# A last chunk of a recurrence and the output projection behind it: two tiles split by token halves, queues reordered

## The chip, the core and the metric

One Trainium2 chip, one of its cores. The metric is the device time of one execution in microseconds (us). TensorE multiplies, VectorE and ScalarE work elementwise and read TensorE's results out of PSUM, GpSimd works on SBUF only, SyncE issues the transfers. Each engine has a queue of its own and takes its instructions strictly in the order in which they are written; between engines only semaphores order the work.

## What is computed

A trunk of two layers on 576 tokens: 64 of a running stream, then 512 of a new one. Cut to the part around the change, for each layer:

```python
proj = rmsnorm(x) @ w_in                     # 1024 -> GLA columns and RWKV columns
o = gla_chunked(q, k, v, log_a, state)       # 4 heads, chunks of 64 tokens, a recurrence over chunks
o = o * rsqrt(mean(o * o) + eps) * gla_norm_w * silu(gg)
y = rwkv7(r, w, k, v, -kk, kk * a, state)    # 8 heads of 64, also a recurrence
y = (y - mean(y)) * rsqrt(var(y) + gn_eps) * ln_w + ln_b
y = (y + bonus) * g
x = x + concat([o, y]) @ w_out               # 1024 -> 1024: the output projection
x = x + conv_ffn(rmsnorm(x))
```

## The kernel before

Everything lies transposed: 128 features on the partitions, the 576 tokens along the free dimension. A dense product takes 128 output features at a time, a tile. Tiles alternate between two slots, s = 0 and 1, each with its weights and its two banks of PSUM (PS[0], PS[1]); a bank holds half of the tokens, HT = 288. Weights and inputs are split into a high and a low part in fp32r, and a product is three passes: high by high, high by low, low by high (`passes`, L610). A pass is two matmuls, one for each half of the tokens (`both`, L600), each with a weight load of its own. For a tile of 8 blocks of the contraction that is 48 matmuls of 288 columns; L602 is the first half's, L603 the second's.

A tile of weights comes by DMA into `raw`; ScalarE makes the high part `whi` when the slot's last tile is done (L1182, semaphore `tile_done`), then GpSimd the low part `wlo` (L529, `w_lo`), and TensorE waits for `w_lo` (`dense`, L619). In the output projection ScalarE does that in `added` (L1200), beside xh and the squares of the next norm, and VectorE adds the tile to x (L2121).

The mixers run in nine chunks of 64 tokens, 0 to 8 (LAST = 8). The loop over i from -1 to 7 does chunk i's recurrence and, beside it, prepares chunk i + 1: the order of all engines' steps in it is written out by hand. A chunk's recurrence of the RWKV heads is a chain in which TensorE and a reader of PSUM alternate, each a group of 16 matmuls of 64 by 64: `carried` (L845, copied by ScalarE to Zc), `solve_z` (L869; VectorE's `add_z`, L1923, makes Z of it and Zc), `carried_y` (L857), `solve_z1` (L879, copied by ScalarE, L1399, to Z1), `solve_z2` (L887; VectorE's `add_rest`, L1939, makes W), `solve_u` (L895, copied to U), and `outputs` (64 matmuls, L903 to L914), from which VectorE makes the new state (`new_state`, L1952 and L1954) and the chunk's y (`add_y`, L1933).

The two norms go by groups of two chunks: a mean on TensorE (the matmul with `mean64` or `mean128`), logarithm and exp on ScalarE, the scale on VectorE (`scale_o`, L1995; `scale_y`, four instructions, L2003). `mixed_o` and `mixed_y` then write the inputs of the output projection: high part mh by ScalarE (L1461, L1470), low part ml by VectorE (L2011, L2017). Blocks 0 to 3 of the contraction are o, 4 to 7 are y. Semaphores `mo_lo` and `my_lo` count groups. For the last group (chunks 7 and 8) y's norm is taken one chunk at a time: `chunk_mean` (L1017) on TensorE, `chunk_centre` (L2030) on VectorE, `square_chunk` (L1475) and `log_chunk` (L1480) on ScalarE, and one exp for both (L1548).

Where exp and logarithm alternate on ScalarE, a table load stands ahead of the one that changes: it is shown with that one's line (L1446 for the exp of `rstd_o`). At the end of the loop's last pass VectorE does `scale_o` of the last group and its product with the silu (L2078); only then do its steps of chunk 8 follow, from L2086 on. TensorE's order behind the loop is:

```python
carried(LAST); solve_z(LAST); chunk_mean(7, mean); carried_y(LAST)
solve_z1(LAST); solve_z2(LAST); solve_u(LAST)
chunk_mean(7, variance); outputs(LAST)
chunk_mean(8, mean); out_part(0, range(0, 1)); chunk_mean(8, variance)
turn_state(St, zb)
out_part(0, range(1, 4)); out_part(1, range(0, 4))
out_part(0, range(4, 8)); out_part(1, range(4, 8))
```

`out_part(s, kts)` (L1079) does blocks kts of tile s for all tokens. Six more tiles follow with `dense`, then the FFN.

## Time and profile before

| | |
|---|---|
| median of 3 runs | 1687.81 us (1686.81 to 1690.52) |
| the profiled execution | 1688.88 us |
| its span | 1686.5 us |
| TensorE: matmuls | 1642.1 us, 97% of the span |
| VectorE | 934.5 us, 55% |
| ScalarE | 660.7 us, 39% |
| GpSimd | 557.8 us, 33% |
| mean granted clock of TensorE | 0.991 of full speed |
| transfers | 115.38 MB, a mean of 68 GB/s |

The profiled execution is 1.07 us above the median; 2.4 us of it lie outside the span. Busy time is that of instructions with an end that is modelled for TensorE, so neighbouring matmuls overlap in the rows: their starts tell the pace. In a timeline row an idle time in brackets stands for the engine's wait just before, with what ended it. The granted clock is a share of TensorE's full speed: 1.00 is 2.4 GHz, 0.50 is 1.2 GHz.

### The profile page before, as it was taken

The page shows a single profiled execution, that of the slowest core. Times are in us where ns is not written, and L with a number is a line of the kernel's source. Part 1 is how long each engine was busy: PE and PEld are TensorE (multiplying, and loading weights), DVE is VectorE, ACT ScalarE, POOL GpSimd, SP SyncE. Part 2 cuts the span into 40 slices and gives each one's busy share as a digit, 9 for nine tenths or more (in the row PEclk, how much of TensorE's full clock was granted, in tenths as well). Part 3 has the DMA queues.
Part 4 walks back from the last instruction along what each step waited for, and adds up shares of the span by engine and source line. Part 5 has one row for each costly group of instructions (what it writes and reads, how often), then busy time and mean ns, then how long its engine had stood idle before and what let it go on. Part 6 is the DMA issues. An engine that isn't in the chain of part 4 may idle for free.

```text
span 1686.5 us, 40380 instructions
## 1 busy us (share of the span) xinstructions
PE 1642.1 (97%) x18045; PEld 1578.2 (94%) x18045; DVE 934.5 (55%) x1414; ACT 660.7 (39%) x995; POOL 557.8 (33%) x293
## 2 busy tenths in 40 slices
PE   7999999989999999999999999999899999999997
PEld 6999988869999999999999998887799999999997
DVE  4669545555566405665546884465556661266643
ACT  5444345553433213333253533555443331233323
POOL 5434311114344333443333432021134433334331
PEclk9999999999999999999999999999899999999999
DMA  5222210002323322223222222000132233232331
GB/s 150 63 75 76 65 40 4 4 2 82 88 75 88 103 73 75 83 81 104 81 74 75 76 76 58 10 4 3 33 88 78 86 94 94 64 88 77 102 88 57
DMA packets 218861, 115.38 MB, mean 68 GB/s; under 512 B 9332, under 2 KB 216450, under 8 KB 218690
## 3 DMA queue, kind: packets, MB, share of 16 engines
q1 hardware_dynamic: 218610, 112.79, 23.5%
q8 instruction: 143, 2.34, 0.6%
q14 instruction: 28, 0.23, 0.0%
q10 hardware_dynamic: 80, 0.02, 0.0%
HBM read 109.27 MB, written 3.53 MB: 67 GB/s over the span
## 4 chain that ended last, share of the span: by engine, by line
PE 94%; ACT 2%; DVE 2%; issue 1%; DMA 0%; POOL 0%; SPq 0%; DVEq 0%; ACTq 0%
PE ps L602 38%; PE ps L603 38%; PE ps L822 2%; PE ps L825 2%; PE ps L819 2%; PE ps L607 1%; PE ps L785 1%; PE ps L798 1%; PE ps L887 1%; PE ps L943 1%; PE ps L799 1%; PE ps L1004 1%; PE ps L879 1%; PE ps L717 1%; PE ps L961 1%
## 5 line engine op out<-in xcount | busy, mean ns | idle before, releaser
L529 POOL TENSOR_TENSOR wlo<-raw,whi 128x1024 fp32r<-128x1024 f32 (+1 forms) x188 | 508.5, 2705 | 861.7 <-ACT whi L1182 861.6
L1182 ACT ACTIVATE whi<-raw 128x1024 fp32r<-128x1024 f32 (+1 forms) x188 | 209.5, 1114 | 650.1 <-PE ps L603 650.1
L602 PE MATMUL ps<-xh,whi 128*128 128x288 f32 x1120 | 332.8, 297 | 4.2 <-DVE xl L1610 4.2
L603 PE MATMUL ps<-xh,whi 128*128 128x288 f32 x1120 | 331.0, 296 | 0.0
L602 PE MATMUL ps<-xl,whi 128*128 128x288 f32 x1120 | 330.2, 295 | 0.0
L603 PE MATMUL ps<-xl,whi 128*128 128x288 f32 x1120 | 329.0, 294 | 0.0
L602 PE MATMUL ps<-xh,wlo 128*128 128x288 f32 x1120 | 329.0, 294 | 0.0
L603 PE MATMUL ps<-xh,wlo 128*128 128x288 f32 x1120 | 328.9, 294 | 0.0
L602 PEld LDWEIGHTS ps<-xh,whi 128*128 128x128 f32 x1120 | 210.7, 188 | 6.2 <-issue 4.5
L603 PEld LDWEIGHTS ps<-xh,whi 128*128 128x128 f32 x1120 | 210.6, 188 | 0.2
L602 PEld LDWEIGHTS ps<-xh,wlo 128*128 128x128 f32 x1120 | 210.7, 188 | 0.0
L603 PEld LDWEIGHTS ps<-xl,whi 128*128 128x128 f32 x1120 | 210.5, 188 | 0.0
L603 PEld LDWEIGHTS ps<-xh,wlo 128*128 128x128 f32 x1120 | 210.1, 188 | 0.0
L602 PEld LDWEIGHTS ps<-xl,whi 128*128 128x128 f32 x1120 | 210.0, 187 | 0.0
L2121 DVE TENSOR_TENSOR x<-x,ps 128x576 f32<-128x576 f32 x48 | 36.2, 753 | 197.4 <-PE ps L603 197.4
L2159 DVE SCALAR_TENSOR_TENSOR cv<-up,par,cv 128x578 f32<-128x578 f32 x44 | 100.5, 2284 | 32.8 <-ACT cv L1566 32.8
L2174 DVE SCALAR_TENSOR_TENSOR hl<-hf,hh 128x576 fp32r<-128x576 f32 x44 | 98.5, 2239 | 33.3 <-ACT hh L1572 33.3
L603 PE MATMUL ps<-hh,whi 128*128 128x288 f32 x352 | 103.7, 295 | 0.0
L603 PE MATMUL ps<-hl,whi 128*128 128x288 f32 x352 | 103.6, 294 | 0.0
L602 PE MATMUL ps<-hl,whi 128*128 128x288 f32 x352 | 103.5, 294 | 0.0
L602 PE MATMUL ps<-hh,wlo 128*128 128x288 f32 x352 | 103.4, 294 | 0.0
L602 PE MATMUL ps<-hh,whi 128*128 128x288 f32 x352 | 103.4, 294 | 0.0
(301 smaller groups left out, 3156.3 us busy)
## 6 DMA issues: line engine op xcount, KB each, us to landing
raw<-in_ffn_w_up SPq DMA_DIRECT2D x88, 512.0 KB, 3.8
raw<-in_w_in SPq DMA_DIRECT2D x52, 512.0 KB, 3.8
raw<-in_ffn_w_down SPq DMA_DIRECT2D x32, 704.0 KB, 4.5
raw<-in_w_out SPq DMA_DIRECT2D x16, 512.0 KB, 3.8
xin<-in_x_prompt SPq DMA_DIRECT2D x4, 512.0 KB, 6.7
out<-xin SPq DMA_DIRECT2D x8, 256.0 KB, 2.9
out<-RW SPq DMA_DIRECT2D x16, 64.0 KB, 2.2
g<-in_rwkv_g SPq DMA_DIRECT2D x2, 256.0 KB, 2.8
```

What stands on the lines that cost most here:

```text
L529: e.tensor_tensor(wlo[s][:, 0:width], raw[s][:, 0:width], whi[s][:, 0:width].bitcast(F32), ALU.subtract).then_inc(w_lo[s], 1)
L602: e.matmul(acc(out)[:, 0], lhsT, rhs[:, 0:HT], start=start, stop=stop)
L603: return e.matmul(acc(out)[:, 1], lhsT, rhs[:, HT:TOK], start=start, stop=stop)
L607: e.matmul(out[:, 0:512], lhsT, rhs[:, 0:512], start=True, stop=True)
L717: ws = e.matmul(PS[2][:, tt], w2a2[0:64, p * P:(p + 1) * P], R[0:64, 12, tt], start=True, stop=True)
L819: mm = e.matmul(powers[h, X, 0], d[h, hp, X, 2], d[h, hp, X, 0], start=True, stop=True)
L822: mm = e.matmul(powers[h, X, 1], d[h, hp, X, 0], d[h, hp, X, 2], start=True, stop=True)
L825: mm = e.matmul(product[h, X], d[h, hp, X, 2], d[h, hp, X, 1], start=True, stop=True)
L1182: e.activation(whi[s][:, 0:width], raw[s][:, 0:width], ACT.Copy).then_inc(w_hi[s], 1)
L2121: e.tensor_tensor(by_half(xt), by_half(xt), acc(PS[s]), ALU.add).then_inc(psum_free[s], 1)
L2159: e.scalar_tensor_tensor(out=cv[:, :], in0=up[:, 1:3 + TOK], scalar=par[:, cw + FF + f:cw + FF + f + 1], in1=cv[:, :], op0=ALU.mult, op1=A ...
L2174: e.scalar_tensor_tensor(out=hl[:, it, :], in0=hf[:, :], scalar=1.0, in1=hh[:, it, :].bitcast(F32), op0=ALU.mult, op1=ALU.subtract).then_i ...
```

## The change

`out_part` becomes `out_half(s, b, kts)`: blocks kts of tile s for token half b alone. The first halves of tiles 1 and 0 are cut into slices that stand between TensorE's steps of chunk 8; behind the turned state only the second halves are left. A first half needs the groups of chunks 0 to 4 alone. The count of y (`Y`) leaves `dv_b` for a semaphore `dv_a` of its own, so that VectorE can make y ahead of the state. VectorE's `scale_o` and its product, and ScalarE's `rstd_o`, move from the end of the loop into the last chunk; the rest of both queues is put in another order there. Squares of chunks 7 and 8 lie in SQ[:, 1], the mean and the variance of chunk 7 in other banks. The diff, cut where only the name of the semaphore changes:

```diff
@@ -110,7 +110,8 @@
 
 PE_B = ["Zc", "Z", "Yc", "Z1", "Z2", "U", "S"]
 AC_B = ["Zc", "Yc", "Z1", "U"]
-DV_B = ["Z", "W", "Sa", "St", "Y"]
+DV_B = ["Z", "W", "Sa", "St"]
+DV_A = ["Y"]
 
 PE_G = ["scores", "tok", "out", "state"]
 AC_G = ["tok", "oE", "oO"]
...
@@ -130,7 +131,7 @@
 LAST = NCH - 1
 PE_E = ["m7", "v7", "m8", "v8"]
 AC_E = ["s7", "l7", "s8", "l8", "rstd"]
-DV_E = ["c7", "y3b", "y3", "gb", "c8", "gy0", "gy1", "gy2", "gy3", "yr", "y"]
+DV_E = ["c7", "c8", "gy0", "gy1", "gy2", "gy3", "gb", "y3b", "y3", "yr", "y"]
 
 
 def program(nc, x_prompt, x_sample, state_gla, state_rwkv, state_rwkv_shift, cache_ffn_conv,
...
@@ -317,7 +318,7 @@
         st_pe = sem("st_pe")
         st_dve = sem("st_dve")
         pe_f, ac_f, dv_f, po_f = sem("pe_f"), sem("ac_f"), sem("dv_f"), sem("po_f")
-        pe_b, ac_b, dv_b = sem("pe_b"), sem("ac_b"), sem("dv_b")
+        pe_b, ac_b, dv_b, dv_a = sem("pe_b"), sem("ac_b"), sem("dv_b"), sem("dv_a")
         pe_g, ac_g, dv_g = sem("pe_g"), sem("ac_g"), sem("dv_g")
         pe_y, ac_y, dv_c, dv_y, po_y = sem("pe_y"), sem("ac_y"), sem("dv_c"), sem("dv_y"), sem("po_y")
         pe_e, ac_e, dv_e, o_last = sem("pe_e"), sem("ac_e"), sem("dv_e"), sem("o_last")
...
@@ -1076,46 +1077,57 @@
                     level(j, 0, 5)
                     level(j, 1, 5)
 
-                def out_part(s, kts):
-
+                def out_half(s, b, kts):
+
+                    groups = l * len(GROUPS) + (3 if b == 0 else len(GROUPS))
+                    if b == 0 and 0 in kts:
+                        pe.wait_ge(w_lo[s], turn(s, l, PAIRS["out"]) + 1)
                     if 0 in kts:
-                        pe.wait_ge(w_lo[s], turn(s, l, PAIRS["out"]) + 1)
-                        pe.wait_ge(mo_lo, (l + 1) * len(GROUPS))
+                        pe.wait_ge(mo_lo, groups)
                     if 4 in kts:
-                        pe.wait_ge(my_lo, (l + 1) * len(GROUPS))
+                        pe.wait_ge(my_lo, groups)
+                    own = slice(b * HT, (b + 1) * HT)
                     for kt in kts:
-                        mm = passes(s, mh, ml, kt, KT)
-                    if KT - 1 in kts:
+                        wh = whi[s][:, kt * P:(kt + 1) * P]
+                        wl = wlo[s][:, kt * P:(kt + 1) * P]
+                        e.matmul(acc(PS[s])[:, b], wh, mh[:, kt, own], start=kt == 0, stop=False)
+                        e.matmul(acc(PS[s])[:, b], wh, ml[:, kt, own], start=False, stop=False)
+                        mm = e.matmul(acc(PS[s])[:, b], wl, mh[:, kt, own], start=False, stop=kt == KT - 1)
+                    if b == 1 and KT - 1 in kts:
                         mm.then_inc(tile_done[s], 1)
 
                 seventh, eighth = slice((LAST - 1) * C, LAST * C), slice(LAST * C, TOK)
-                squares = SQ[:, 0, :].rearrange("p (a t) -> p a t", t=2 * C)
+                squares = SQ[:, 1, :].rearrange("p (a t) -> p a t", t=2 * C)
                 carried(LAST)
                 solve_z(LAST)
-                front(dv_f, DV_F, LAST, "L5A")
-                back(dv_b, DV_B, LAST - 1, "Y")
-                chunk_mean(7, bank(2)[:, 0:256], R[:, 0:4, seventh])
+                back(dv_a, DV_A, LAST - 1, "Y")
+                chunk_mean(7, bank(5)[:, 256:512], R[:, 0:4, seventh])
                 carried_y(LAST)
                 solve_z1(LAST)
+                front(dv_f, DV_F, LAST, "L5A")
+                out_half(1, 0, range(0, 2))
                 solve_z2(LAST)
+                out_half(1, 0, range(2, 4))
                 solve_u(LAST)
+                out_half(1, 0, range(4, 6))
+                outputs(LAST)
                 ending(ac_e, AC_E, "s7")
-                chunk_mean(7, bank(2)[:, 256:512], squares[:, :, 0:C])
-                outputs(LAST)
-                back(dv_b, DV_B, LAST, "Y")
+                chunk_mean(7, gb[:, 256:512], squares[:, :, 0:C])
+                out_half(1, 0, range(6, 7))
+                back(dv_a, DV_A, LAST, "Y")
                 pe.wait_ge(ac_o, nth(AC_O, (l + 1) * len(GROUPS) - 1, "oln"))
                 chunk_mean(8, pb[:, 0:256], R[:, 0:4, eighth])
+                out_half(1, 0, range(7, 8))
                 back(ac_b, AC_B, LAST, "Zc")
-                out_part(0, range(0, 1))
+                out_half(0, 0, range(0, 1))
                 ending(ac_e, AC_E, "s8")
                 chunk_mean(8, pb[:, 256:512], squares[:, :, C:2 * C])
+                out_half(0, 0, range(1, 8))
                 back(dv_b, DV_B, LAST, "St")
                 turn_state(St, zb)
-                out_part(0, range(1, 4))
-                ending(ac_e, AC_E, "l7")
-                out_part(1, range(0, 4))
-                out_part(0, range(4, 8))
-                out_part(1, range(4, 8))
+                for kts in (range(0, 4), range(4, 8)):
+                    for s in range(2):
+                        out_half(s, 1, kts)
                 for it in range(1, KT // 2):
                     for s in range(2):
                         dense(s, turn(s, l, PAIRS["out"] + it), mh, ml, KT)
...
@@ -1528,24 +1540,24 @@
                     copy_powers(j, 1, 4)
                     if i == LAST - 1:
                         log_o(po_)
-                        rstd_o(po_)
 
                 seventh, eighth = slice((LAST - 1) * C, LAST * C), slice(LAST * C, TOK)
-                squares = SQ[:, 0, :].rearrange("p (a t) -> p a t", t=2 * C)
+                squares = SQ[:, 1, :].rearrange("p (a t) -> p a t", t=2 * C)
                 copy_carried(LAST)
                 copy_carried_y(LAST)
+                copy_back(LAST, "Z1", Z1[:, :, :], zb[:, 256:512])
+                rstd_o(N_Y)
                 rstd_y(N_Y - 1)
-                copy_back(LAST, "Z1", Z1[:, :, :], zb[:, 256:512])
+                copy_back(LAST, "U", U[:, :, :], zb[:, 256:512])
+                ac.wait_ge(dv_o, (l + 1) * len(GROUPS))
+                square_chunk("7", R[:, 0:4, seventh], squares[:, :, 0:C])
                 mixed_o(N_Y)
-                ac.wait_ge(dv_y, nth(DV_Y, (l + 1) * N_Y - 1, "yn3"))
-                square_chunk("7", R[:, 0:4, seventh], squares[:, :, 0:C])
-                copy_back(LAST, "U", U[:, :, :], zb[:, 256:512])
-                log_chunk("7", bank(2)[:, 256:512], squares[:, :, 0:C])
+                log_chunk("7", gb[:, 256:512], squares[:, :, 0:C])
                 square_chunk("8", R[:, 0:4, eighth], squares[:, :, C:2 * C])
-                mixed_y(N_Y - 1)
                 log_chunk("8", pb[:, 256:512], squares[:, :, C:2 * C])
                 ac.wait_ge(ac_e, nth(AC_E, l, "l8"))
-                e.activation(SQ[:, 0, :], SQ[:, 0, :], ACT.Exp, scale=-0.5).then_inc(ac_e, 1)
+                e.activation(SQ[:, 1, :], SQ[:, 1, :], ACT.Exp, scale=-0.5).then_inc(ac_e, 1)
+                mixed_y(N_Y - 1)
                 mixed_y(N_Y)
 
                 added(l, PAIRS["out"], l * NORMS + 1, KT * P, KT * P)
...
@@ -1927,10 +1939,10 @@
                     y = by_pair(R[:, 0:4, bass.ds(i * C, C)])
                     step(pe_b, PE_B, i, "S")
                     if i == 1:
-                        e.tensor_copy(y, from_rows(0)).then_inc(dv_b, 1)
+                        e.tensor_copy(y, from_rows(0)).then_inc(dv_a, 1)
                     else:
                         step(ac_b, AC_B, i, "Yc")
-                        e.tensor_tensor(y, by_pair(Yc), from_rows(0), ALU.add).then_inc(dv_b, 1)
+                        e.tensor_tensor(y, by_pair(Yc), from_rows(0), ALU.add).then_inc(dv_a, 1)
 
                 def add_rest(i):
 
...
@@ -2070,40 +2082,38 @@
                     new_gla_state(j)
                     add_power(j, 0, 5)
                     add_power(j, 1, 5)
-                    if i == LAST - 1:
-                        scale_o(po_)
-                        dv.wait_ge(silu_done, (l + 1) * NP)
-                        dv.wait_ge(dv_o, (l + 1) * len(GROUPS))
-                        cc = group(po_)[1]
-                        e.tensor_tensor(G[:, 4:8, cc], G[:, 4:8, cc], G[:, 8:12, cc], ALU.mult).then_inc(o_last, 1)
 
                 seventh, eighth = slice((LAST - 1) * C, LAST * C), slice(LAST * C, TOK)
-                chunk_centre("7", bank(2)[:, 0:256], seventh)
+                add_z(LAST)
+                chunk_centre("7", bank(5)[:, 256:512], seventh)
+                add_rest(LAST)
+                scale_o(N_Y)
+                dv.wait_ge(silu_done, (l + 1) * NP)
+                dv.wait_ge(dv_o, (l + 1) * len(GROUPS))
+                cc = group(N_Y)[1]
+                e.tensor_tensor(G[:, 4:8, cc], G[:, 4:8, cc], G[:, 8:12, cc], ALU.mult).then_inc(o_last, 1)
+                add_y(LAST)
                 scale_y(N_Y - 1)
-                add_z(LAST)
-                add_rest(LAST)
+                chunk_centre("8", pb[:, 0:256], eighth)
                 mixed_o(N_Y)
                 act("g3")
-                cc = group(N_Y - 1)[1]
-                dv.wait_ge(dv_y, nth(DV_Y, (l + 1) * N_Y - 1, "yn3"))
-                e.tensor_tensor(R[:, 0:4, cc], R[:, 0:4, cc], BV[:, :, cc], ALU.add).then_inc(dv_e, 1)
-                mine("y3b")
-                e.tensor_tensor(R[:, 0:4, cc], R[:, 0:4, cc], gate[:, :, cc], ALU.mult).then_inc(dv_e, 1)
-                new_state(LAST)
-                add_y(LAST)
-                cc = group(N_Y)[1]
-                e.tensor_tensor(BV[:, :, cc], BV[:, :, cc], gate[:, :, cc], ALU.mult).then_inc(dv_e, 1)
-                chunk_centre("8", pb[:, 0:256], eighth)
                 dv.wait_ge(ac_e, nth(AC_E, l, "s8"))
                 for p in range(NP):
                     e.scalar_tensor_tensor(out=R[:, p, cc], in0=R[:, p, cc], scalar=pcol("ln_w", p),
                                            in1=gate[:, p, cc], op0=ALU.mult, op1=ALU.mult).then_inc(dv_e, 1)
-                mixed_y(N_Y - 1)
+                e.tensor_tensor(BV[:, :, cc], BV[:, :, cc], gate[:, :, cc], ALU.mult).then_inc(dv_e, 1)
+                new_state(LAST)
+                c3 = group(N_Y - 1)[1]
+                dv.wait_ge(dv_y, nth(DV_Y, (l + 1) * N_Y - 1, "yn3"))
+                e.tensor_tensor(R[:, 0:4, c3], R[:, 0:4, c3], BV[:, :, c3], ALU.add).then_inc(dv_e, 1)
+                mine("y3b")
+                e.tensor_tensor(R[:, 0:4, c3], R[:, 0:4, c3], gate[:, :, c3], ALU.mult).then_inc(dv_e, 1)
                 dv.wait_ge(ac_e, nth(AC_E, l, "rstd"))
                 mine("gy3")
-                e.tensor_tensor(R[:, 0:4, cc], R[:, 0:4, cc], pair3(SQ[:, 0, :], 2 * C), ALU.mult).then_inc(dv_e, 1)
+                e.tensor_tensor(R[:, 0:4, cc], R[:, 0:4, cc], pair3(SQ[:, 1, :], 2 * C), ALU.mult).then_inc(dv_e, 1)
                 mine("yr")
                 e.tensor_tensor(R[:, 0:4, cc], R[:, 0:4, cc], BV[:, :, cc], ALU.add).then_inc(dv_e, 1)
+                mixed_y(N_Y - 1)
                 mixed_y(N_Y)
                 dv.wait_ge(states_out, l * 128 + 64)
                 step(dv_g, DV_G, LAST, "Sg")
```

## Rows read from the trace of the kernel before

**Rows 1.** Timeline, layer 0, end of the loop and first solve (start, duration, what).

```profile
356.23 1.28 ACT L1446 ACT_TABLE_LOAD   x1
356.92 0.48 DVE L1914 TENSOR_TENSOR work<-work,ps 128x128 f32<-128x128 f32 x2
357.25 0.70 PE L1017 MATMUL ps<-RW,mean 128*128 128x256 f32 x2
357.53 0.63 ACT L1446 ACTIVATE work<-work 128x512 f32<-128x512 f32 x1
357.88 0.68 PE L857 MATMUL ps<-RW,work 64*64 64x64 f32 x16
358.19 0.75 DVE L1995 SCALAR_TENSOR_TENSOR G<-G,par,work 128x512 f32<-128x512 f32 x1 [0.79 <-ACT work L1446]
...
359.99 1.13 DVE L2003 SCALAR_TENSOR_TENSOR RW<-RW,par,work 128x128 f32<-128x128 f32 x4
361.04 0.41 DVE L1923 TENSOR_TENSOR work<-work,ps 128x256 f32<-128x256 f32 x1
361.50 0.80 PE L879 MATMUL ps<-work 64*64 64x64 f32 x16 [2.94 <-DVE work L1923]
```

**Rows 2.** Windows: stretch, its length, busy time of each engine, granted clock.

```profile
358.60:361.50 2.90, 0.00 (x0) 0.00 (x0) 2.75 (x8) 0.90 (x2) 0.00 (x0) 1.00 0.00 0
361.50:365.50 4.00, 2.99 (x49) 2.50 (x49) 1.56 (x3) 1.21 (x3) 0.00 (x0) 0.55 0.00 0
...
1184.50:1184.80 0.30, 0.00 (x0) 0.00 (x0) 0.30 (x2) 0.00 (x0) 0.00 (x0) 0.56 0.00 0
```

**Rows 3.** Timeline of TensorE: a solve of chunk 8, then steps of the loop.

```profile
362.78 1.12 PE L887 MATMUL ps<-work 64*64 64x64 f32 x16 [0.48 <-ACT work L1399]
...
1160.82 0.66 PE L869 MATMUL ps<-work 64*64 64x64 f32 x16
...
1161.29 0.60 PE L857 MATMUL ps<-RW,work 64*64 64x64 f32 x14
...
1172.61 0.27 PE L903 MATMUL ps<-work 64*64 64x64 f32 x1
...
1173.75 0.66 PE L943 MATMUL ps<-ident,G 128*64 128x128 f32 x8
```

**Rows 4.** Timeline: end of the first output tile, start of the third, both layers.

```profile
381.89 1.06 ACT L1182 ACTIVATE whi<-raw 128x1024 fp32r<-128x1024 f32 x1 [5.01 <-PE ps L603]
...
383.03 2.39 POOL L529 TENSOR_TENSOR wlo<-raw,whi 128x1024 fp32r<-128x1024 f32 x1 [35.34 <-ACT whi L1182]
...
385.47 0.40 PE L602 MATMUL ps<-mh,whi 128*128 128x288 f32 x1 [0.45 <-POOL wlo L529]
...
1211.37 0.40 PE L602 MATMUL ps<-mh,whi 128*128 128x288 f32 x1 [0.46 <-POOL wlo L529]
```

**Rows 5.** Timeline of TensorE, layer 0: from a group of 16 to output matmuls.

```profile
372.24 0.68 PE L757 MATMUL ps<-ident,work 64*64 64x64 f32 x16
372.85 0.41 PE L602 MATMUL ps<-mh,whi 128*128 128x288 f32 x1
373.09 0.29 PE L603 MATMUL ps<-mh,whi 128*128 128x288 f32 x1
```

**Rows 6.** Chain that ended last, layer 1 (start, its time on the chain, what).

```profile
1196.14 0.24 PE ps L603
```

**Rows 7.** Timeline of VectorE, layer 0: the last low part.

```profile
376.91 0.69 DVE L2017 TENSOR_TENSOR ml<-RW,mh 128x512 fp32r<-128x512 f32 x1 [0.70 <-ACT mh L1470]
```

**Rows 8.** Waits of TensorE: us in total, times, longest us.

```profile
PE ps L1013 <- ACT work L1427: 3.6, 2, 1.8
PE ps L1156 <- DVE Tall L1619: 2.4, 1, 2.4
```

**Rows 9.** Windows at the end of the program, columns as in rows 2.

```profile
1676.00:1676.20 0.20, 0.20 (x4) 0.20 (x3) 0.00 (x0) 0.20 (x1) 0.00 (x0) 0.65 0.00 0
...
1679.40:1679.60 0.20, 0.20 (x2) 0.00 (x0) 0.20 (x1) 0.20 (x1) 0.00 (x0) 0.82 0.93 348
```

8 lines of the change are left out of this document (4 added, 4 removed).

## The prediction

> **What bounds the kernel now.** I read the page first, then TensorE's waits, then the timeline of the last chunk in layer 0, then the granted clock there. Layer 1 repeats layer 0 about 824.4 us later (the profile shows two such places, one for each layer). TensorE works nearly all the time, so a gain must fill its holes, and the last chunk has the largest.
>
> The head of that hole is in [rows 1]. The chunk's first solve, L879, can't start before 361.50, after 2.94 us of idle. It waits for VectorE's L1923, the sum into Z. But L1923 has nothing late of its own: VectorE had finished the last power (L1914) at 357.40, and then stood in line behind the GLA scale (L1995, from 358.19, itself released by ScalarE's exp), the product with the silu, one centring, and the four scalings of L2003. None of these is an input of Z. The reader is to see a queue order, not a dependency.
>
> [Rows 2] show what else the idle time brings. The granted clock is full in the idle stretch and 0.55 right behind it: TensorE falls from 2.4 to 1.2 GHz about when the chain begins. In layer 1 it has fallen by 1184.8, and at 1196 the output matmuls still come 0.24 us apart, against 0.13 at the full clock [rows 5, 6]. So the chunk's steps, each waited for by the next, run at half speed: a 16-matmul group lasts 1.12 us in L887, and 0.66 us as L869 at the full clock [rows 3].
>
> [Rows 4] are the other end. The first output tile is done at 381.89 (ScalarE starts the next split then), GpSimd has the low part from 383.03, and TensorE starts the third tile at 385.47, 3.58 us after 381.89. In layer 1 it starts at 1211.37, which is 386.95 on layer 0's time: 1.48 us later, for the longer stay at the low clock. These two starts are my yardstick; behind them is dense work whose order doesn't change.
>
> **The change, worked out on layer 0's time, at the full clock.** Prices of a group: 0.47 us from one group of 16 to the next (L869 to L857), 1.14 us for `outputs` (L903 to L943), both [rows 3]; a 256-column mean 0.63 us (L1017 to L857, [rows 1]). A slice of six output matmuls behind a group of 16: from L757 to the first L602 0.61 us, then 0.24, then 0.13 each [rows 5], so 1.5 us, and I add 0.1 us for the way back to 64-row matmuls, which no row shows alone. Bounds of that: nothing, and the 0.3 us more than the spacing that the way in costs. I take 0.1 because small groups at full clock follow each other without a visible hole.
>
> 1. *Queues of the head.* VectorE's add_z comes straight behind L1914, at 357.4, and ends at 357.8. ScalarE's Zc copy is no longer behind the exp either. TensorE goes through the mean of chunk 7 and `carried_y` as before and reaches the solve at 357.88 + 0.47 = 358.35 instead of 361.50. Gain 3.15 us; the deferred work isn't free and is costed below.
> 2. *Slices in the chain.* Group plus slice of six takes 1.6 us, three times: second solve 359.95, third 361.55, `outputs` 363.15. Without slices the step would wait for the engine between (VectorE's L1923 takes 0.41 us; I price ScalarE's copy of the same width at 0.4, since twice the width takes 0.63), so a slice lengthens a step by some 0.7 us, but takes 0.8 us of output work from the end.
> 3. *ScalarE between them.* Z1 copied by 359.45, then the moved exp of the GLA norm with its table load: 1.30 us from load to exp and 0.63 for the exp [rows 1], 361.4; the second exp, 362.0; U is solved at 362.2 and copied by 362.65. TensorE comes for it at 363.15: hidden, with 0.5 us to spare.
> 4. *VectorE.* The moved scale and product (0.75 and 0.69) run from 361.4 to 362.85, while VectorE waits for `outputs`. They cost nothing as long as that cover stands; without it 1.4 us would fall on add_y.
> 5. *Means and single slices.* `outputs` to 364.3, variance of chunk 7 to 364.95, slice of three 365.55, mean of chunk 8 366.2. VectorE: add_y 364.9, then the four scalings (1.13) 366.0, centring 366.65; ScalarE squares it by 367.1. TensorE meanwhile does six matmuls (1.0 us) to 367.2, the variance to 367.85, then 21 matmuls to 370.8, the state turn 371.4.
> 6. *New waits.* The state turn now waits for a state that VectorE makes behind mixed_o, four scalings and a product: 366.65 + 0.69 + 1.13 + 0.69 + 0.84 = 370.0. Behind that wait all the rest of TensorE's queue stands; it is met with 0.8 us. The last half needs the second norm: log 368.4, load and exp 370.3, VectorE's six wide operations (two for chunks 5 and 6, two for the end, two low parts) at 0.69 [rows 7], with ScalarE's copy between: 374.15. TensorE wants it at 371.4 + 0.3 + 24 x 0.13 = 374.9. Met by 0.7 us.
> 7. *The tail.* Only the second token half is left, 48 matmuls against 90 now. But tile 0 is finished only 12 matmuls (1.58 us) ahead of tile 1, not 24, so it covers less of the split: tile 0 done at 371.4 + 0.3 + 36 x 0.132 = 376.45, third tile 3.58 us later at 380.03, with TensorE idle for 2.0 us where it idles 0.46 now [rows 4]. The second split is GpSimd's at once after the first and is hidden by the third tile, whose 48 matmuls take 6.3 us.
> 8. *DMA and the other queues.* No transfer is added or taken. SP's state stores and the weight loads behind them keep their order; GpSimd waits in front of the first split for over 35 us today [rows 4]. Waits on the split-off Y counter are met at the same instants in the loop. Nothing.
>
> **Sum.** Layer 0: 385.47 - 380.03 = 5.4 us. Layer 1: 386.95 - 380.03 = 6.9 us. Together 12.4 us. The profiled execution took 1688.88 us (its span 1686.5): 1676.5 us. The median of the runs is 1.07 us lower, so I forecast **1675.4 us**. With no switch costs the line of TensorE would be some 1.2 us shorter per layer (1673.0).
>
> A price disputed: [rows 1] show the table load at 356.23 and the exp at 357.53, 1.30 us together. The Trainium skill, page "ScalarE: Activation LUTs", section "What ACT_TABLE_LOAD costs", gives about 2.66 us for each switch, with a drain of 1.38 us behind the load. It speaks against this change, which puts a load ahead of the U copy: by it U would be copied at 363.8, `outputs` start 0.7 us later, and the sum would be 11.0 us, 1676.8 us by its figure as an estimate.
>
> **Rivals.**
> - *The clock falls behind the new idle time.* TensorE idles 1.8 us at L1013 and 2.4 us at L1156 [rows 8]. The first leaves the clock full; after the second it drops at about 1676.1 and comes back at 1679.4 [rows 9], though TensorE worked in between. The predicted hole of 2.0 us lies between them. Price: 3.4 us at half speed under dense work, 1.7 us per layer: 1677.1 with one layer, 1678.8 with both. For it: the head of layer 1 fell after less idle time. Against: what surrounds the hole is unbroken dense work.
> - *The last half waits for the norm as today.* The last low part is done at 377.60 in layer 0 today [rows 7]. If the reordered VectorE work (item 6) lets it end there again, TensorE stands still before the last 24 matmuls: 377.6 + 1.58 + 3.58 = 382.8. Gain 2.7 us in layer 0 and 4.2 in layer 1: 1681. Against: the chain that feeds it starts 3.15 us earlier and runs at the full clock.
> - *Slower: the clock falls all the same, with slices on the chain.* Place: before the first solve, in both layers. Price: dense spacing 0.24 us instead of 0.13, groups of 16 some 0.4 us longer, means 0.5, `outputs` 0.65 (the group's 1.12 against 0.66 applied to each). To the state turn: three group-and-slice steps +3.0, `outputs` +0.65, three means +1.5, 30 slice matmuls +3.3, turn +0.3, so +8.8 us; the last 48 add 5.3: 14 us per layer, 1704 us in all. It decides from about 6 us per layer, which means the low clock from the solve to beyond the variance of chunk 8. For: in layer 1 the fall came at 1184.5 [rows 2], 1.5 us after `carried_y` (358.56 on layer 0's time). Against: the slices are there just where TensorE stood still.
> - *Nothing gained.* The slices only fill time that the chain then takes longer, and the end stays: about 1687.8. It needs both the clock and the queue order to have been harmless, which [rows 1, 2] speak against.
>
> **How the numbers follow.** Forecast as summed 0.50 (1673 to 1677); clock behind the hole 0.22; last half late 0.15; nothing gained 0.06; slower 0.07. The range takes the first three: low end the sum without switch costs and 1 us for timing that no row shows, 1672; high end the late half with one loss of clock, 1683. A measurement of this kernel can tell about 0.2%, 3.4 us, from no change. The first three cases are all beyond it: faster 0.87, same 0.06, slower 0.07.
>
> **What would show it.** In the changed profile: L879's successor within 0.1 us of `carried_y`, granted clock 1.00 from the first solve to the last output slice; slices of six between the solves and `outputs` about 363.2; the third tile about 380.0 in layer 0 and at the same place in layer 1 (the 1.5 us between the layers gone); TensorE waiting about 2 us for GpSimd's low part. Wrong if: granted clock below 1.00 between the solves; TensorE waiting for VectorE's state or for the last low part; or the layers' gains summing to less than 8 us.

## The result, and the profile after

The changed kernel takes **1676.49 us**, the median of 4 runs (1673.0 to 1677.52). The kernel before took 1689.16 us beside it (4 runs, 1686.81 to 1690.58). The ratio is 0.9923 [0.9903, 0.9943]: 12.7 us faster by the medians, where 12.4 were forecast. The profiled execution took 1677.05 us, its span 1675.2; the forecast for it was 1676.5.

From the page of the changed kernel: span and busy time of each engine.

```profile
span 1675.2 us, 40378 instructions
PE 1641.4 (98%) x18045; PEld 1579.6 (94%) x18045; DVE 937.3 (56%) x1414; ACT 662.5 (40%) x995; POOL 558.1 (33%) x293
```

No engine does less than before: TensorE has the same 18045 matmuls and 1641.4 us of busy time, against 1642.1. What went is its idle time.

Timeline of the changed kernel, layer 0, the chain of chunk 8 (start, duration, what; columns as in [rows 1]):

```profile
356.85 0.70 PE L1018 MATMUL ps<-RW,mean 128*128 128x256 f32 x2
357.48 0.68 PE L858 MATMUL ps<-RW,work 64*64 64x64 f32 x16
358.00 0.63 PE L880 MATMUL ps<-work 64*64 64x64 f32 x16
358.56 0.40 PE L1093 MATMUL ps<-mh,whi 128*128 128x288 f32 x1
359.08 1.28 ACT L1458 ACT_TABLE_LOAD   x1
359.55 0.68 PE L888 MATMUL ps<-work 64*64 64x64 f32 x16
360.38 0.63 ACT L1458 ACTIVATE work<-work 128x512 f32<-128x512 f32 x1
361.15 0.68 PE L896 MATMUL ps<-work 64*64 64x64 f32 x16
361.88 0.39 ACT L1411 ACTIVATE work<-ps 128x256 f32<-128x256 f32 x1 [0.35 <-PE ps L896]
362.75 0.34 PE L904 MATMUL ps<-work 64*64 64x64 f32 x8
363.84 0.70 PE L1018 MATMUL ps<-work,mean 128*128 128x256 f32 x2
364.78 0.59 PE L1018 MATMUL ps<-RW,mean 128*128 128x256 f32 x2
366.34 0.70 PE L1018 MATMUL ps<-work,mean 128*128 128x256 f32 x2 [0.18 <-ACT work L1487]
369.74 0.68 PE L758 MATMUL ps<-ident,work 64*64 64x64 f32 x16
```

The first solve (L880, L879 before) stands 1.15 us behind the mean of chunk 7 (L1018, L1017 before), where [rows 1] have 4.25. Between L880, L888, L896 and L904 the steps are 1.55 to 1.60 us, with six output matmuls of L1093 to L1095 in each. The only wait of TensorE in this stretch is the 0.18 us at 366.34.

The end of the first tile, in both layers (timeline of the changed kernel; the last two rows are the start of the third tile and are to be laid beside [rows 4]):

```profile
371.50 1.48 DVE L2029 TENSOR_TENSOR ml<-RW,mh 128x512 fp32r<-128x512 f32 x2
...
375.46 1.06 ACT L1194 ACTIVATE whi<-raw 128x1024 fp32r<-128x1024 f32 x1 [3.21 <-PE ps L1095]
...
379.00 0.40 PE L603 MATMUL ps<-mh,whi 128*128 128x288 f32 x1 [1.98 <-POOL wlo L530]
...
1198.02 0.40 PE L603 MATMUL ps<-mh,whi 128*128 128x288 f32 x1 [1.99 <-POOL wlo L530]
```

And the granted clock (windows of the changed kernel, columns as in [rows 2]): two of the chain in each layer's last chunk, then two from just behind the start of the third tile.

```profile
358.00:369.70 11.70, 11.52 (x172) 10.24 (x168) 7.53 (x20) 9.11 (x14) 0.00 (x0) 1.00 0.01 3
1176.00:1188.70 12.70, 12.52 (x184) 10.92 (x184) 8.39 (x22) 9.10 (x14) 0.00 (x0) 1.00 0.01 3
...
379.50:382.00 2.50, 2.50 (x12) 2.50 (x12) 2.50 (x2) 0.00 (x0) 2.29 (x1) 0.50 0.72 204
1199.00:1201.50 2.50, 2.50 (x12) 2.50 (x12) 2.50 (x2) 0.00 (x0) 1.81 (x1) 0.50 0.75 210
```

In the chain the clock is now at 2.4 GHz all the way, where [rows 2] show 0.55. But right behind the third tile's start it is at 1.2 GHz, for 3.4 us in each layer. That is the first rival, which had a chance of 0.22, and it came in both layers of this execution.

**Where the time went.** I measure between two marks, so that differences earlier in the execution drop out: from the mean of chunk 7 to the start of the third tile. Before: 28.22 us in layer 0 and 29.70 in layer 1. After: 22.15 and 22.16. So the changed stretch gives back 6.07 and 7.54 us, 13.6 together; the clock behind the holes takes back some 1.5 us per layer (measured under change_again below). That makes 10.5 us for the change itself. The two spans differ by 11.3: the rest lies outside the changed stretch (layer 0 began 0.4 us earlier, layer 1's mixers were 0.9 us shorter, the end of the program took 0.5 more) and is no work of the change. Stays at 1.2 GHz also come outside that stretch, in one trace and not in the next: one from 345.2 us in this trace, one from 1163.4 in tail_serial's. They are part of why executions of one kernel differ.

### The profile page after: what moved, and what is told of

Read it like the earlier page. It is cut to its first block, busy times and chain, and to the rows that moved or that the text cites. A ratio compares the mean times of both kernels' runs of the same rounds, so it can differ in the third digit from the quotient of the medians.

```text
span 1675.2 us, 40378 instructions
## 1 busy us (share of the span) xinstructions
PE 1641.4 (98%) x18045; PEld 1579.6 (94%) x18045; DVE 937.3 (56%) x1414; ACT 662.5 (40%) x995; POOL 558.1 (33%) x293
## 4 chain that ended last, share of the span: by engine, by line
PE 96%; ACT 2%; DVE 1%; issue 0%; POOL 0%; DMA 0%; ACTq 0%; DVEq 0%
PE ps L603 37%; PE ps L604 37%; PE ps L823 2%; PE ps L826 2%; PE ps L820 2%; PE ps L608 1%; PE ps L786 1%; PE ps L799 1%; PE ps L888 1%; PE ps L944 1%; PE ps L800 1%; PE ps L1005 1%; PE ps L718 1%; PE ps L962 1%; PE ps L880 1%; PE ps L870 1%
## 5 line engine op out<-in xcount | busy, mean ns | idle before, releaser
L1194 ACT ACTIVATE whi<-raw 128x1024 fp32r<-128x1024 f32 (+1 forms) x188 | 209.8, 1116 | 642.7 <-PE ps L604 636.3
```

The source lines that it names most:

```text
L1194: e.activation(whi[s][:, 0:width], raw[s][:, 0:width], ACT.Copy).then_inc(w_hi[s], 1)
```

## The experiments

All numbers are medians with the range of the runs; ratios are to the kernel before on the same chip. "Distance" is the one above, from the mean of chunk 7 to the third tile, layer 0 and layer 1. Edits are to the changed kernel except where the text says otherwise.

| kernel | median us (range, runs) | ratio [95%] | distance | low clock behind the third tile's start |
|---|---|---|---|---|
| change | 1676.49 (1673.0 to 1677.52, 4) | 0.9923 [0.9903, 0.9943] | 22.15 / 22.16 | both layers |
| change_again | 1676.28 (1676.0 to 1678.12, 5) | 0.993 [0.9917, 0.9942] | 22.12 / 22.14 | layer 1 |
| tail_serial | 1673.67 (1672.68 to 1673.8, 4) | 0.9909 [0.9895, 0.9924] | 21.64 / 21.64 | no |
| tail_weave | 1672.68 (1672.19 to 1673.63, 4) | 0.9905 [0.9891, 0.992] | 21.63 / 21.62 | no |
| tail_weave_again | 1672.05 (1671.12 to 1672.56, 4) | 0.9914 [0.99, 0.9927] | 21.62 / 21.62 | no |
| queues_only | 1691.0 (1684.98 to 1693.89, 10) | 1.001 [0.9998, 1.0021] | 28.30 / 29.18 | both |
| queues_lead48 | 1683.43 (1680.65 to 1685.33, 11) | 0.9977 [0.9968, 0.9986] | 28.6 / 27.2 | no hole |
| norm_back | 1681.02 (1678.48 to 1684.41, 4) | 0.9955 [0.9938, 0.9972] | 23.99 / 24.00 | no |
| before_lead12 | 1692.66 (1690.08 to 1698.25, 11) | 1.0024 [1.0015, 1.0033] | 30.62 / 30.60 | no |
| pool_serial | 1675.43 (1673.72 to 1679.18, 5) | 0.9926 [0.9912, 0.9939] | 22.20 / 22.18 | no |
| pool_weave | 1675.05 (1673.62 to 1680.93, 5) | 0.9926 [0.9913, 0.994] | 22.19 / 22.18 | no |
| turn_last | 1676.81 (1675.48 to 1677.27, 5) | 0.9942 [0.9928, 0.9956] | 22.24 / 22.24 | layer 0 |
| turn_mid | 1672.29 (1671.11 to 1672.82, 4) | 0.9891 [0.9874, 0.9907] | 21.01 / 20.98 | no |

### Does the hole cost the clock? tail_serial and tail_weave

tail_serial finishes tile 0's last half before tile 1's is begun:

```diff
-                for kts in (range(0, 4), range(4, 8)):
-                    for s in range(2):
+                for s in range(2):
+                    for kts in (range(0, 4), range(4, 8)):
                         out_half(s, 1, kts)
```

> Changed kernel, with the four second-half pieces at the end in the order tile 0 blocks 0-3, tile 0 blocks 4-7, tile 1 blocks 0-3, tile 1 blocks 4-7, so that tile 0 is finished 24 matmuls ahead of tile 1 instead of 12. Theory A (the 2.0 us of idle time in front of the third tile cost twice: as idle time, and by the 3.3 us at half clock right behind them): TensorE waits about 1.0 us for the last low part, tile 0 is done at about 374.7 instead of 375.4, the third tile starts at about 378.2 instead of 379.0 after only about 0.5 us of idle time, and the granted clock stays at 1.00; 2.3 us per layer, 4.7 in all, so about 1671.8 us against 1676.5 for the change. Theory B (the clock falls there for another reason, such as the mixed work of the chain before it): the clock still falls behind the third tile's start, and only the 0.7 us per layer are gained, about 1675.1 us.

Timeline of tail_serial, layer 0: the two waits of the tail, for VectorE's low part and for the split.

```profile
372.99 0.40 PE L1093 MATMUL ps<-mh,whi 128*128 128x288 f32 x1 [0.83 <-DVE ml L2029]
...
378.46 0.40 PE L603 MATMUL ps<-mh,whi 128*128 128x288 f32 x1 [0.41 <-POOL wlo L530]
```

The hole of 2.0 us is split into one of 0.83 and one of 0.41, the clock stays at 1.00 behind both, and the third tile comes 0.5 us earlier per layer. The median falls by 2.8 us. Twice 0.5 is 1.0; that leaves 1.8, about the price of one fall of the clock per execution. So the clock behaved as in theory A, but its 1671.8 us did not come: the shorter hole is worth 0.5 us per layer and not 0.7, and two falls in each execution were counted where fewer come.

tail_weave fills the first wait with two blocks of tile 1:

```diff
-                for kts in (range(0, 4), range(4, 8)):
-                    for s in range(2):
-                        out_half(s, 1, kts)
+                for s, kts in ((0, range(0, 4)), (1, range(0, 2)), (0, range(4, 8)), (1, range(2, 4)), (1, range(4, 8))):
+                    out_half(s, 1, kts)
```

> Changed kernel, with the second-half pieces in the order tile 0 blocks 0-3, tile 1 blocks 0-1, tile 0 blocks 4-7, tile 1 blocks 2-7: tile 0 leads by 18 matmuls. Theory A: almost no wait for the last low part (needed at about 372.8, there at 373.0), tile 0 done at about 374.7, third tile at about 378.2 after 1.2 us of idle time; 1.2 us is less than the 1.8 us that left the clock full in the loop, so the clock stays at 1.00: about 1671.8 us, like the serial order. Theory B: clock falls all the same, about 1675.1 us. If 1.2 us are enough for a fall, this one shows it and the serial order does not.

Timeline of tail_weave, layer 0, start of the third tile.

```profile
377.70 0.40 PE L603 MATMUL ps<-mh,whi 128*128 128x288 f32 x1 [1.20 <-POOL wlo L530]
```

The wait for the low part is gone and all idle time is in front of the third tile, 1.20 us in each layer; the clock doesn't fall behind it, as theory A had it. The distance is that of tail_serial: tile 0 ends 18.07 us behind the mean of chunk 7 in both, since the low part sets it. tail_weave was run again later on another chip:

> The woven tail once more, unaltered, beside the one with the turn last, as its measure: about 1672.7 us, spread about 1.5 us, no fall of the clock.

Its 8 runs in all lie between 1671.12 and 1673.63 us, the 9 of the change between 1673.0 and 1678.12. So an order of the tail's blocks is worth 3 to 4 us to the change: some 4 by the medians, 3 by the ratios to the kernel before on each one's chip.

### How often does the clock fall? change_again

> The changed kernel once more, unaltered, on the chip and in the rounds of the variants beside it. In its first four runs it took 1673.0 to 1677.5 us; the two tail variants took 1672.2 to 1673.8. Theory A (a fall of the clock behind the 2.0 us hole comes in some executions and some layers only, as in the profile of the kernel with the norm put back, which had the hole and no fall) expects a spread of some 3 to 4 us again with a median near 1676, and single runs down to about 1673. Theory B (the fall is fixed by the program) expects a spread of about 1.5 us, as the tail variants have.

The changed kernel once more, unedited. The holes of 2.0 us are there in both layers; the clock fell behind the second alone. Start of the third tile in both layers, then ScalarE's next split behind that tile (L1194 again), then the granted clock of each stretch (columns as in [rows 2]):

```profile
379.85 0.40 PE L603 MATMUL ps<-mh,whi 128*128 128x288 f32 x1 [1.98 <-POOL wlo L530]
...
1197.07 0.40 PE L603 MATMUL ps<-mh,whi 128*128 128x288 f32 x1 [1.99 <-POOL wlo L530]
...
386.50 1.06 ACT L1194 ACTIVATE whi<-raw 128x1024 fp32r<-128x1024 f32 x1 [1.17 <-PE ps L604]
...
1205.25 1.06 ACT L1194 ACTIVATE whi<-raw 128x1024 fp32r<-128x1024 f32 x1 [2.72 <-PE ps L604]
...
380.20:383.60 3.40, 3.40 (x28) 3.40 (x27) 3.40 (x3) 0.00 (x0) 2.47 (x1) 1.00 0.58 154
1198.60:1202.00 3.40, 3.40 (x16) 3.40 (x15) 2.55 (x2) 0.81 (x2) 1.27 (x1) 0.50 0.63 190
```

The third tile takes 6.65 us in layer 0 and 8.18 in layer 1: a fall costs 1.5 us. In the first trace of the change the two layers take 8.19 and 8.17. The runs spread over 2.1 us, which lies between the two theories; it is the traces that decide for the first.

Over all traces with a hole of 2.0 us in front of the third tile it fell behind 5 of 10 (change 2 of 2, change_again 1 of 2, queues_only 2 of 2, norm_back and before_lead12 none of 4). It fell behind none of the fourteen of 1.20 us or less there (tail_serial, both runs of tail_weave, pool_serial, pool_weave, turn_mid, and the kernel before). So the loss is not there each time, which an all-or-nothing forecast for it could not show.

### What is the queue order worth without the slices? queues_only and queues_lead48

queues_only takes the seven slices out of the chain and puts their work behind the state turn:

```diff
...
-                out_half(1, 0, range(0, 2))
...
-                out_half(0, 0, range(1, 8))
                 back(dv_b, DV_B, LAST, "St")
                 turn_state(St, zb)
+                out_half(0, 0, range(0, 8))
+                out_half(1, 0, range(0, 8))
```

> Changed kernel without its slices: the first halves of tiles 0 and 1 (48 matmuls) stand behind the turned state, ahead of the second halves; ScalarE's and VectorE's new order is kept. Theory A (the new queue order brings the head 3.1 us forward and keeps the clock, but most of the gain of a layer is the 6.3 us of output work done in the holes): first solve at about 358.0, step from solve to solve about 1.1 us, outputs held to about 362.3 by ScalarE's U copy, state turn about 369.0 in place of 369.7, third tile about 384.3 in layer 0 in place of 379.0, about 5.2 us per layer worse than the change: 1687 us. Theory B (queue order alone is the gain and the slices are padding): within 2 us per layer of the change, 1680 us or less. If the clock falls between the solves without the slices, some 3 to 4 us per layer more than theory A, about 1694 us.

Waits of TensorE in queues_only (us in total, times, longest), then windows in layer 0 just behind the wait for the state and just behind the third tile's start.

```profile
PE ps L603 <- POOL wlo L530: 4.0, 2, 2.0
...
PE ps L758 <- DVE work L1961: 3.7, 2, 1.9
...
PE ps L888 <- ACT work L1406: 3.2, 10, 0.6
...
PE ps L1018 <- ACT work L1482: 2.5, 2, 1.2
...
PE ps L904 <- ACT work L1406: 1.5, 2, 0.8
```

```profile
369.00:370.00 1.00, 1.00 (x15) 0.88 (x12) 0.97 (x3) 0.28 (x1) 0.00 (x0) 0.50 0.00 0
386.00:387.00 1.00, 1.00 (x5) 1.00 (x6) 1.00 (x2) 0.00 (x0) 1.00 (x1) 0.50 0.09 27
```

The head is as early as in the change, and nothing is left of the gain. The chain now waits at each step, 1.9 us for the state alone. The clock falls right behind that wait in layer 0 and within it in layer 1, and again behind the hole in both. Expected were 5.2 us per layer more than the change, 1687 us, with the clock held in the chain. Since this kernel differs from the change by the slices alone, with the same head and the same tail, its distances give their worth: 6.15 us in layer 0 and 7.02 in layer 1, nearly all that the change gains. It shows the price of a slice too: the solves stand 1.20 us apart (358.66, 359.87, 361.07 in its timeline), against 1.60 with a slice that takes 0.8 us. A slice lengthens the step by half of what it does.

Was it the new tail alone that ate the gain? queues_lead48 keeps the chain bare, but does all 48 matmuls of tile 0 and then all of tile 1 (the slices go as in queues_only):

```diff
...
+                out_half(0, 0, range(0, 8))
+                for s, b, kts in ((0, 1, range(0, 8)), (1, 0, range(0, 8)), (1, 1, range(0, 8))):
+                    out_half(s, b, kts)
```

> The changed kernel's queues without its slices, as in queues_only, but with the output matmuls behind the turned state in the order all of tile 0, then all of tile 1, so that tile 0 leads by 48 matmuls and its split is covered. Theory A (the queue order is worth about 3 us per layer by itself, which queues_only lost again to the 2.0 us hole and to the clock): no wait for GpSimd's low part, third tile 24.9 us behind the mean of chunk 7 (28.3 in queues_only, 28.2 and 29.7 before) where the clock holds, 26.6 where it falls in the wait for the state; 1680 to 1684 us. Rival (the order of the queues is worth nothing without the slices, as the 1691 us of queues_only reads at first sight): 1688 us or more.

Window of queues_lead48, layer 0, in the chain.

```profile
363.00:365.00 2.00, 2.00 (x64) 1.88 (x58) 0.69 (x2) 1.60 (x3) 0.00 (x0) 0.50 0.00 0
```

The split is covered (no wait for GpSimd at the third tile) and the kernel is 4.3 us faster than the one before beside it, but the chain still loses the clock. In layer 0 it falls at 362.6 us already, behind waits of 0.57, 0.52 and 0.76 us, and again in the wait for the state. So the median came where it was expected, but the distances did not: 28.6 and 27.2 us, where 24.9 or, with one fall, 26.6 were forecast. They are 0.4 us longer and 2.5 shorter than the kernel before, 2.1 us together; the rest of the 4.3 lies outside the edited stretch and is not explained. The queue order alone, with the tail covered, is thus worth 2 to 4 us.

### What do the slices bring without the moved norm? norm_back

```diff
                         log_o(po_)
+                        rstd_o(po_)
...
-                rstd_o(N_Y)
...
+                        scale_o(po_)
...
-                scale_o(N_Y)
```

(The product with the silu goes back with the scale.)

> Changed kernel with the exp, the scale and the product of the last GLA group put back to the end of the loop, ahead of add_z; slices and all else as in the change. Theory A (the long idle time before the first solve is what takes TensorE to 1.2 GHz, and slices then stand on the chain at the low clock): first solve at about 361, granted clock 0.50 behind it for at least 3.4 us, third tile 3.1 + 2.5 = 5.6 us per layer later: about 1687.7 us. Rival (the slices keep TensorE busy enough that the clock does not fall): only the 3.1 us per layer, about 1682.7 us.

Timeline of norm_back, layer 0, VectorE's queue in front of the first solve.

```profile
361.90 0.75 DVE L2007 SCALAR_TENSOR_TENSOR G<-G,par,work 128x512 f32<-128x512 f32 x1 [0.79 <-ACT work L1458]
362.75 0.69 DVE L2090 TENSOR_TENSOR G<-G 128x512 f32<-128x512 f32 x1
363.36 0.41 DVE L1935 TENSOR_TENSOR work<-work,ps 128x256 f32<-128x256 f32 x1
363.69 0.42 DVE L2042 SCALAR_TENSOR_TENSOR RW<-ps,RW 128x256 f32<-128x256 f32 x1
363.83 0.68 PE L880 MATMUL ps<-work 64*64 64x64 f32 x16 [1.64 <-DVE work L1935]
```

The head waits 1.64 us again, not the 2.94 of [rows 1]: the other 1.3 us were the centring and the four scalings of L2003, which stay behind the sum here. The third tile comes 1.84 us later per layer, where I had expected 3.1. The clock doesn't fall in the chain at all, as the rival had it: with slices behind it, the idle head of 1.64 us did not cost the clock in either layer of this trace. By medians norm_back is 4.5 us slower than the change and 7.9 faster than its kernel before. (This execution was already some 4 us late at the mean of chunk 7 of layer 0; that is outside the edit, and the distances don't hold it.)

### The lead of tile 0 in the kernel before: before_lead12

Here the edit is to the kernel before. It finishes tile 0 only 12 matmuls ahead of tile 1, as the change does:

```diff
-                out_part(0, range(4, 8))
-                out_part(1, range(4, 8))
+                out_part(0, range(4, 6))
+                out_part(1, range(4, 6))
+                out_part(0, range(6, 8))
+                out_part(1, range(6, 8))
```

> The kernel before, with only the last two pieces of tiles 0 and 1 interleaved in blocks of two (tile 0 blocks 4-5, tile 1 blocks 4-5, tile 0 blocks 6-7, tile 1 blocks 6-7), so that tile 0 leads tile 1 by 12 matmuls instead of 24: the tail's shortened cover without the rest of the change. Theory A: tile 0 done 1.58 us later, idle time in front of the third tile 2.0 us instead of 0.46, third tile 1.58 us later per layer (layer 0: 387.05), and where the clock falls behind it 1.6 us more: 3.2 to 6.4 us slower than the kernel before, about 1693.5. Rival (the split's latency is hidden elsewhere and the lead does not matter): no change, about 1689 us.

It is 4.1 us slower, and the hole is 2.0 us in both layers, 1.5 more than in [rows 4]. The distances grow by 2.40 and 0.90 us, 3.3 together: twice 1.5 for the hole, while the stays at 1.2 GHz in the two chains nearly cancel (3.4 us longer in layer 0, 3.4 shorter in layer 1). The lost lead is a real cost, which the change carries along.

### Can the norm be made earlier? pool_serial and pool_weave

After tail_serial the low part of the last norm sets the end of tile 0. I moved the bonus sum and the gate product of chunks 5 and 6, two wide operations, from VectorE to GpSimd, which is idle there:

```diff
                     e.tensor_tensor(R[:, 0:4, cc], R[:, 0:4, cc], gate[:, :, cc], ALU.mult).then_inc(po_y, 1)
...
+                finish_y(N_Y - 1)
...
-                e.tensor_tensor(R[:, 0:4, c3], R[:, 0:4, c3], BV[:, :, c3], ALU.add).then_inc(dv_e, 1)
-                mine("y3b")
-                e.tensor_tensor(R[:, 0:4, c3], R[:, 0:4, c3], gate[:, :, c3], ALU.mult).then_inc(dv_e, 1)
```

> The serial tail, and the bonus sum and the gate product of chunks 5 and 6 moved from VectorE to GpSimd, behind its other such groups; it has nothing to do there. Theory A (the 0.8 us that TensorE waits for the last low part in the serial tail is VectorE's queue: six wide operations in a row): VectorE is done about 0.7 us earlier, wait down to about 0.3 us, third tile about 0.5 to 0.7 us earlier per layer: about 1672.4 us against 1673.7 for the serial tail. Rival (the low part is held by ScalarE's exp and copies, or GpSimd and VectorE slow each other on their shared port): no gain, or a loss of up to 1 us per layer.

Timeline of pool_serial, layer 0, VectorE and GpSimd beside each other.

```profile
365.27 1.27 POOL L575 TENSOR_TENSOR RW<-RW,Tall 128x512 f32<-128x512 f32 x1 [18.22 <-DVE RW L2016]
365.42 1.67 DVE L2024 TENSOR_TENSOR ml<-G,mh 128x512 fp32r<-128x512 f32 x1
366.62 1.52 POOL L577 TENSOR_TENSOR RW<-RW,cum 128x512 f32<-128x512 f32 x1
367.02 2.06 DVE L2103 SCALAR_TENSOR_TENSOR RW<-RW,par,cum 128x128 f32<-128x128 f32 x4
...
370.52 0.68 PE L759 MATMUL ps<-ident,work 64*64 64x64 f32 x16 [1.05 <-DVE work L1967]
```

Timeline of tail_serial, layer 0: the same two operations with GpSimd idle.

```profile
365.71 0.68 DVE L2023 TENSOR_TENSOR ml<-G,mh 128x512 fp32r<-128x512 f32 x1
366.35 1.15 DVE L2102 SCALAR_TENSOR_TENSOR RW<-RW,par,cum 128x128 f32<-128x128 f32 x4
```

The low part takes 1.67 us for 0.68, the four scalings 2.06 for 1.15. VectorE loses 1.9 us on these two for the 1.4 that were taken from it; the state comes late and TensorE waits 1.05 us for it. The times fit a VectorE that stood still until GpSimd's operation ended: that one ends at 366.54, the low part 0.55 us later at 367.09, though it had begun at 365.42. By medians the kernel is 1.8 us slower than tail_serial, where 1.3 less were expected; the third tile comes 0.56 us later per layer. The rival had that, a loss of up to 1 us per layer. pool_weave, the same edit with one block of tile 1 between tile 0's halves, fares the same.

> As the one with the two operations on GpSimd, but with tile 1 block 0 between tile 0's two pieces: three matmuls (0.4 us) in the wait for the low part. Theory A: no wait for the low part, idle time in front of the third tile about 0.8 us, clock stays at 1.00; third tile at the same place as in the serial order, about 1672.2 us, 0.5 to 1 us below the woven tail alone (1672.7). Rival as there: no gain over the woven tail.

### Moving the state turn: turn_last and turn_mid

In both, VectorE makes the new state behind the last low part. turn_last also puts the turn behind all output matmuls:

```diff
-                back(dv_b, DV_B, LAST, "St")
-                turn_state(St, zb)
...
+                for s, kts in ((0, range(0, 4)), (1, range(0, 2)), (0, range(4, 8)), (1, range(2, 4)), (1, range(4, 8))):
+                    out_half(s, 1, kts)
+                back(dv_b, DV_B, LAST, "St")
+                turn_state(St, zb)
...
-                new_state(LAST)
...
+                new_state(LAST)
```

> The woven tail, with the turn of the last state put behind the last output piece on TensorE, and VectorE's two operations for that state behind the last low part. Theory A (what now holds the tail is VectorE's queue up to the last low part, in which the state takes 0.84 us, and the turn can stand in the hole behind the last piece): low part about 0.8 us earlier, third tile about 20.8 us behind the mean of chunk 7 instead of 21.63, idle time in front of it about 0.9 us: 1.6 us in all, about 1671.0 us. Rival (the low part is held by ScalarE's exp): third tile within 0.3 us of where it was, 1672.5 us, with the turn only filling the hole.

Timeline of turn_last, layer 0.

```profile
377.31 0.42 DVE L2033 COPY RW<-ps 128x256 f32<-128x256 f32 x1 [3.98 <-PE ps L758]
...
379.09 0.58 PE L603 MATMUL ps<-mh,whi 128*128 128x288 f32 x1 [1.84 <-DVE x L2130]
```

A miss of 5.8 us: the low part did come 0.6 us earlier, but VectorE's copy of the turned state stands in its queue ahead of the sum that empties tile 0's accumulator (L2130). It waits 3.98 us for the late turn, and the third tile for the sum. It is the fault that the change mends at the head, made anew at the tail. turn_mid puts the turn right behind tile 0's last block instead:

```diff
+                    if s == 0 and 4 in kts:
+                        back(dv_b, DV_B, LAST, "St")
+                        turn_state(St, zb)
```

> As the kernel with the turn last, but the turn of the state stands right behind tile 0's last piece, ahead of tile 1's. Theory A (turn_last lost its gain because VectorE's copy of the turned state stands ahead of its sum for tile 0, so that the third tile waited 1.8 us for that sum and not for the weights): VectorE's copy is done before tile 0 is added late enough to matter, the third tile waits for GpSimd's low part again, at about 21.0 us behind the mean of chunk 7 against 21.63 in the woven tail; about 1671.2 us against 1672.4. Rival (the delayed state costs in another place, too): 1673 us or more.

Timeline of turn_mid, layer 0, start of the third tile.

```profile
378.34 0.40 PE L603 MATMUL ps<-mh,whi 128*128 128x288 f32 x1 [0.40 <-POOL wlo L530]
```

The distance is 21.0 us as expected, 0.6 less per layer than tail_weave's, and the hole is down to 0.40. Its median of 1672.29 is 17.3 us below its kernel before, but can't be told from tail_weave's 1672.05 and 1672.68. By the medians both beat the change by some 4 us and the kernel before by about 1%.

## Why the prediction was right, and where it was not

The working was made with the mean of chunk 7 at 357.25; this execution has it at 356.85, so I add 0.40 us to the trace's times before I compare.

1. *Queues of the head*: right. Solve forecast 358.35, came at 358.40.
2. *Slices in the chain*: right. 359.95, 361.55 and 363.15 were forecast and came so to the hundredth. The row that no trace showed, 0.1 us for the way back, was good. Only its aside was wrong: by queues_only the bare step is 1.20 us, so a slice lengthens it by 0.4 us, not by "some 0.7".
3. *ScalarE between them*: right. U's copy ends at 362.27 in the trace, 362.67 on the forecast's time for 362.65, and L904 takes it 0.5 us later. The price in dispute is settled by the rows: the load starts at 359.08 and the exp at 360.38, 1.30 us. The Trainium skill ("ScalarE: Activation LUTs", "What ACT_TABLE_LOAD costs") gives 2.66 us for the switch; by that, as an estimate, this exp would stand at about 361.7 and U's copy some 1.0 us later, since ScalarE waited 0.35 us for U. The measurement differs and decides.
4. *VectorE's moved work*: hidden, as said. norm_back gives its price without the cover: 1.84 us per layer.
5. *Means and single slices*: too dear. The variance of chunk 7 was forecast for 364.3 and came at 364.24, but the mean of chunk 8 at 365.18 (365.55), its variance at 366.74 (367.2), the turn at 370.14 (370.8). The step that failed is the price of a slice behind a mean. I took it as behind a group of 16, with the 0.24 us of the first step and the 0.1 us of the way back: 0.60 us for three matmuls and 1.0 for six, on top of a mean's 0.65. But a mean is made of 128-row matmuls like the slice, and mean and slice of three take 0.94 us, not 1.25; with a slice of six it is 1.38, not 1.65. That makes 0.63 us per layer at the third tile: 379.40 for 380.03.
6. *New waits*: none, as said. The last low part ended at 373.38 (forecast 374.15) and was wanted at 374.06 (374.9): met by 0.7 us, as forecast. The only wait in the chain is 0.18 us for ScalarE's square of chunk 8.
7. *The tail*: right in mechanism and size: idle 2.0 us were forecast, 1.98 came. tail_serial, tail_weave and before_lead12 show that the short lead is the cause.
8. *DMA*: nothing, as said. TensorE's one long wait for a transfer is 5.1 us for the last norm's rows in both kernels.

The difference between the layers is gone, 22.15 and 22.16 us, as the text had it. The sum is off in two terms of opposite sign. The chain was 0.63 us per layer shorter than worked out. The clock behind the hole cost some 1.5 us per layer in this execution (1.7 was the rival's price), and I had given the case 0.22. It should have been counted in part: over ten holes of that size it came five times. The chain's two layers give 1.2 us more than forecast, and one fall per execution takes 1.5 back. So the mechanism was right, but that 12.7 us by the medians stand so near the forecast 12.4 is in part luck.

The rival of the late norm was wrong here but close: in tail_serial, where tile 0 wants the low part earlier, TensorE does wait 0.83 us for it. The slower case had the slices at 1.2 GHz; no trace with slices in the chain shows a low clock there, and queues_only and queues_lead48, without them, both do. The slices carry the gain: taken out alone they cost 13.2 us by the distances, of the 13.6 (the prices overlap: the moved norm, taken back alone, costs 3.7). The queue order without them is worth 2 to 4 us, and only with another tail. The slices do work in the steps' waits and keep the clock up; how these two divide was not tried apart.

## What to carry to other kernels

Read the queue of an engine that others wait for and ask of each instruction in it who needs it: 2.94 us of idle time was work in line ahead of a short sum, and turn_last made the same mistake again. Independent matmuls between the steps of a recurrence cost half of their time here and keep the clock up, but each reorder of the last tiles must be checked for the lead of a tile over the split that refills its slot (1.06 and 2.4 us here). A hole of 2 us in front of dense work can cost another 1.5 through the clock; a hole of 1.2 us, or one of 0.8 and one of 0.4, did not. In a bare chain of small steps even waits under 0.8 us did not keep the clock safe.

## What the runs showed of the hardware

- TensorE's clock fell to 1.2 GHz behind 5 of 10 idle stretches of 2.0 us in front of the third tile and behind one of turn_last's two of 1.84, with the same kernel in one layer and not in the other, and behind none of fourteen of 1.2 us or less. Each fall there lasted 3.4 us under dense work and cost 1.5 us.
- Behind the idle head of 2.94 us, or within it, it fell in 4 of 4 (the kernel before and before_lead12), behind one of 1.64 us with slices after it in none of 2 (norm_back). In the bare chain of queues_lead48, layer 0, it fell with no wait over 0.76 us since the first solve.
- GpSimd at work on SBUF slows VectorE on SBUF: 0.68 to 1.67 us for a 128x512 operation, 1.15 to 2.06 us for four of 128x128 (tail_serial and pool_serial). Work given to the idle engine made the busy one later.
